# A two-block transformer kernel: merged norms and early context columns, the first expert's products ahead of the gates, squares summed by TensorE, and a store in four parts

## The chip, the core and the metric

The kernel runs on one core of one Trainium2 chip. PE is TensorE (matrix products into PSUM banks), ACT is ScalarE, DVE is VectorE, POOL is GpSimd and SP is SyncE; the last two mostly issue DMAs. The metric is the device time of one execution in microseconds, lower is better. The time before is 1702.18 us, the median of three runs (1700.3 to 1703.35).

## What is computed

A first block over 256 tokens of width 1024, then a second block over these tokens and 256 context tokens. Cut to what matters here:

```python
def rmsnorm(x, g):                       # EPS = 1e-6
    return x * rsqrt(mean(x * x) + EPS) * g

# first block
u = rmsnorm(h, norm_mix); proj = u @ w_in
o_a = forgetting_attention(...); o_b = stick_breaking_attention(...)
h = h + concat(rmsnorm(o_a, norm_fox_out), rmsnorm(o_b, norm_sb_out)) @ w_out
h = h + memory_cross_attention(rmsnorm(h, norm_xattn), rmsnorm(mem, norm_mem))   # 4 heads
h = h + moe(rmsnorm(h, norm_ffn))        # 16 experts of hidden 256: 4 groups of 4,
                                         # best group, 2 best experts in it, all computed
x = rmsnorm(h, norm_final)               # "fin1"

# second block, two layers; the last one needs its output on x alone
for l in range(2):
    shift, scale, gate (two of each) = silu(c) @ w_mod[l] + b_mod[l]       # for x
    the same of c_ctx                                                      # for ctx
    h  = modulate(rmsnorm(x,  g_norm1[l]), sh1,  sc1)     # h*(1+scale)+shift
    hc = modulate(rmsnorm(xc, g_norm1[l]), sh1c, sc1c)
    project both with w_in[l]: Fourier mix, mLSTM (q, k, v, o, gates), latent attention
    ...
    x = x + ga1 * (mix @ w_out[l]); x = x + ga2 * mlp(modulate(rmsnorm(x, g_norm2[l]), ...))
out = rmsnorm(x, g_final)                # "fin2"
```

## The kernel before

Activations are kept transposed: partitions hold 128 of the 1024 features, eight tiles of them, and columns are tokens. `LAT` are the 256 columns of the tokens, `CTX` the 256 of memory or context; the residual `res` holds both. Each engine has its own program, written out by hand; the order in each is the order of the code, and semaphores join them.

Weights come from HBM in 350 pieces of 512 KB over SP's queue into a ring of four slots. Each product is made of three: ACT rounds the piece to `wh` (L532), DVE makes the remainder `wl` (L1568, `split`), and the activations have the same two parts `uh` and `ul`. PE (L995, through `prod`) sums uh*wh, ul*wh and uh*wl.

A norm goes so: ACT squares tiles of `res` (L558) into slots of `sq`, the first into slot 3 and the others in turn into slots 0 and 1; DVE adds each to slot 3 (`add_square`, L1586); PE multiplies slot 3 by a matrix of ones (`norm`), which sums over partitions, with f32 operands; ACT makes the reciprocal root `rstd` by Ln and Exp (L568, L570). Then DVE forms the tiles `uv` (L1608), ACT rounds them to `uh` (L578), and DVE makes the rest `ul` (L1597 or L1599). Around some norms PE has filler matmuls on a tile of ones (`turn_over`, L1039); the table `SPIN` holds their counts before and after each norm.

The modulation vectors are products of one column with a weight matrix. DVE makes them in 48 tiles for layer 0 as dots (L1676 and L1681, `mod_tiles`; each tile is one dot for the context and one for the tokens) of a tile that POOL has loaded. Six stand in the stick-breaking attention, four in the output projection (`MOD_OUT`), four in the cross-attention's query (`MOD_XQ`), two in its output (`MOD_XO`), and 32 in the expert loop, one for each of the 32 half-experts (units).

The router: ACT copies the logits (L717), PE transposes them (L1276), DVE works out the weights, PE spreads them over the partitions with 64 matmuls (`gates`) into two banks that ACT empties (L727), and then the first unit begins. In each unit PE makes gate and up (48 matmuls), and the down product of the unit before.

The hand-over: after the last unit DVE adds four banks to the residual (L1914), adds the bias of the modulation (L1920, L1923), scales the residual by fin1 (L1931), and layer 0's first norm `n1_0` follows over tokens and context. Then PE computes three outputs side by side (`together`): the gates of the mLSTM and its first two heads, 24 steps of three matmuls each, 512 columns wide. ACT copies the head (L793).

In each layer the scans of the mLSTM's gates (`gate_rows`) stand in DVE's program at the third and fourth of the projection's tiles. At the end DVE scales eight tiles (L2266) and SP stores them in one DMA:

```python
            sp.wait_ge(S("norm_out"), normed("fin2")[1])
            sp.dma_start(out, res[:, :, LAT]).then_inc(S("stored"), 16)
```

## Time and profile before

| | us |
|---|---|
| median of 3 runs | 1702.18 |
| the profiled execution | 1705.07 |
| its span in the trace | 1703.2 |
| PE busy | 1619.8 |
| DVE busy | 1077.3 |
| ACT busy | 771.8 |
| POOL busy | 96.6 |

The profiled execution is one run of its own: 1703.2 us of span and 1.87 us around it. A timeline lists what one engine did in order: start, length, engine, line, operation, output<-inputs, how many alike, and in brackets the idle time before with the operation that ended it. Matmuls are pipelined, so the length of one is more than its step to the next: the step is read from two starts. PEclk is the granted clock of PE, 1.00 being 2.4 GHz and 0.50 being 1.2 GHz.

### The profile page before, as it was taken

What the parts mean: (1) busy time and instruction counts of PE and PEld (TensorE: products, weight loads), DVE (VectorE), ACT (ScalarE), POOL (GpSimd) and SP (SyncE); (2) the same over time, 40 slices, a digit from 0 to 9 for tenths busy, and PEclk for the clock granted to TensorE, in tenths of its full rate; (3) what the DMA queues carried; (4) which work ended last, traced back from release to release, by engine and by line L of the source; (5) the groups of instructions that cost most, each with busy time, mean ns of one, the idle gap of its engine ahead of it and who ended that gap; (6) DMA issues with size and microseconds to landing.
All of it is one profiled execution on the core that took longest, in us unless ns stands there. A gap on an engine that the chain in (4) does not pass through costs nothing.

```text
span 1703.2 us, 27364 instructions
## 1 busy us (share of the span) xinstructions
PE 1619.8 (95%) x9992; PEld 1396.6 (82%) x9992; DVE 1077.3 (63%) x1800; ACT 771.8 (45%) x1306; POOL 96.6 (6%) x160
## 2 busy tenths in 40 slices
PE   7999988999999999999889999999999898899997
PEld 7988567899999996775668788888887785799997
DVE  5544677658888887932584755555556944765554
ACT  5544444444444445343462642134323354665562
POOL 0000100000000000000020000000000000100000
PEclk9999999999999999999999999999999999999998
DMA  7633435337777770332114355455542351155552
GB/s 286 203 121 106 119 121 197 126 106 245 244 246 246 244 236 25 99 123 63 34 29 136 136 189 177 142 165 189 166 145 91 112 158 30 45 166 186 173 184 86
DMA packets 70841, 250.96 MB, mean 147 GB/s; under 512 B 7760, under 2 KB 10976, under 8 KB 70640
## 3 DMA queue, kind: packets, MB, share of 16 engines
q1 hardware_dynamic: 54000, 189.43, 33.9%
q0 software_dynamic: 16768, 60.54, 12.5%
q8 instruction: 49, 0.80, 0.2%
q14 instruction: 24, 0.20, 0.0%
HBM read 248.84 MB, written 1.09 MB: 147 GB/s over the span
## 4 chain that ended last, share of the span: by engine, by line
PE 81%; DVE 12%; ACT 3%; issue 3%; DMA 1%; DVEq 0%; SPq 0%; ACTq 0%
PE pair L995 79%; DVE uv L1608 1%; DVE sq L2086 1%; DVE wl L1568 1%; ACT wh L532 1%; DVE sq L1586 1%; DVE small L1635 1%; DVE sq L1644 1%; PE pair L1162 1%; PE pair L1039 1%; DVE uh_f L1681 1%; ACT sq L558 0%; ACT sq L600 0%; DVE ul L1597 0%; DVE spent L1676 0%
## 5 line engine op out<-in xcount | busy, mean ns | idle before, releaser
L995 PE MATMUL pair<-uh,wh 128*128 128x256 f32 (+3 forms) x1840 | 579.0, 315 | 13.1 <-DVE ul L1597 4.5
L1568 DVE TENSOR_TENSOR wl<-ring,wh 128x1024 fp32r<-128x1024 f32 x350 | 426.9, 1224 | 245.0 <-ACT wh L532 237.9
L995 PE MATMUL pair<-uh,wl 128*128 128x256 f32 (+3 forms) x1840 | 574.3, 312 | 0.0
L995 PE MATMUL pair<-ul,wh 128*128 128x256 f32 (+3 forms) x1840 | 572.7, 311 | 0.0
L532 ACT ACTIVATE wh<-ring 128x1024 fp32r<-128x1024 f32 x350 | 367.5, 1052 | 267.9 <-PE pair L995 262.3
L995 PEld LDWEIGHTS pair<-uh,wh 128*128 128x128 f32 (+1 forms) x1840 | 343.5, 187 | 42.6 <-issue 13.8
L995 PEld LDWEIGHTS pair<-uh,wl 128*128 128x128 f32 (+1 forms) x1840 | 343.6, 187 | 25.6
L995 PEld LDWEIGHTS pair<-ul,wh 128*128 128x128 f32 (+1 forms) x1840 | 343.3, 187 | 24.9
L995 PE MATMUL pair<-hh,wh 128*128 128x512 f32 (+1 forms) x512 | 172.7, 337 | 0.8
L995 PE MATMUL pair<-hh,wl 128*128 128x512 f32 (+1 forms) x512 | 172.0, 336 | 0.0
L995 PE MATMUL pair<-hl,wh 128*128 128x512 f32 (+1 forms) x512 | 172.0, 336 | 0.0
L995 PEld LDWEIGHTS pair<-hh,wh 128*128 128x128 f32 x512 | 97.1, 190 | 12.0 <-issue 2.0
L995 PEld LDWEIGHTS pair<-hl,wh 128*128 128x128 f32 x512 | 97.2, 190 | 10.0
L995 PEld LDWEIGHTS pair<-hh,wl 128*128 128x128 f32 x512 | 97.1, 190 | 10.0
L2207 DVE TENSOR_TENSOR hl<-sq,hh 128x512 f32 (+1 forms) x64 | 35.8, 559 | 95.9 <-ACT hh L954 95.8
L949 ACT ACTIVATE sq<-pair 128x512 f32<-128x512 f32 (+1 forms) x64 | 31.3, 489 | 107.4 <-PE pair L995 107.4
L995 PE MATMUL pair<-hidh,wl 128*128 128x256 f32 x256 | 72.6, 284 | 0.0
L995 PE MATMUL pair<-hidh,wh 128*128 128x256 f32 x256 | 72.5, 283 | 0.0
L995 PE MATMUL pair<-hidl,wh 128*128 128x256 f32 x256 | 72.4, 283 | 0.0
L1039 PE MATMUL pair<-spin 128*128 128x512 f32 x250 | 65.9, 414 | 0.0
L995 PE MATMUL pair<-wh,uh 128*128 128x256 f32 (+1 forms) x192 | 57.2, 298 | 3.0 <-ACT qkp L793 3.0
L471 POOL DMA_DIRECT2D uh_f<-in_mods x48 | 36.0, 751 | 418.1 <-DVE macc L1681 267.4
(259 smaller groups left out, 2080.7 us busy)
## 6 DMA issues: line engine op xcount, KB each, us to landing
ring<-in_w_stream SPq DMA_DIRECT2D x350, 512.0 KB, 3.9
uh_f<-in_mods POOLq DMA_DIRECT2D x48, 512.0 KB, 6.1
mod_w<-in_mods POOLq DMA_DIRECT2D x48, 512.0 KB, 3.8
ml<-ml_dram POOLq DMA_DIRECT2D x4, 512.0 KB, 8.1
table<-in_table SPq DMA_DIRECT2D x1, 1849.5 KB, 12.0
res<-in_x SPq DMA_DIRECT2D x4, 256.0 KB, 3.9
res<-in_mem SPq DMA_DIRECT2D x1, 1024.0 KB, 14.3
res<-in_ctx POOLq DMA_DIRECT2D x1, 1024.0 KB, 6.1
```

Of the source, the lines that this page charges most:

```text
L471: pool.dma_start(mod_w[l][g % 2], src).then_inc(S(f"mod_in{g % 2}"), 16)
L532: act.activation(wh[:, s, :], ring[:, s, :], ACT.Copy).then_inc(S("w_hi"), 1)
L949: act.activation(r, bank[(b0 + j) % 4][:, 0:n], ACT.Relu).then_inc(S("job_emptied_act"), 1)
L995: ins = pe.matmul(*operands, **flags)
L1039: pe.matmul(bank[b], spin[:, 0:P], spin[:, :], start=True, stop=True)
L1162: last = pe.transpose(bank[6][:, to * P:(to + 1) * P], prob[i % 2][:, j * P:(j + 1) * P], ident)
L1568: tt(wl[:, s, :], ring[:, s, :], wh[:, s, :].bitcast(F32), ALU.subtract).then_inc(S("w_lo"), 1)
L1586: tt(sq[0:p, 3, 0:n], sq[0:p, 3, 0:n], sq[0:p, t % 2, 0:n], ALU.add).then_inc(S("norm_add"), 1)
L1608: last = stt(o, src, g, r, ALU.mult, ALU.mult)
L1635: dve.tensor_reduce(smv(i, 0, 0, g), b, AX_X, ALU.max, negate=True).then_inc(S("sm_max"), 1)
L1644: last = ts(p, p, smv(i, 1, k), None, ALU.mult)
L2207: tt(hl[:, d, 0:n].rearrange("p a b -> p (a b)"), sq[:, 2 + j % 2, 0:n], hh[:, d, 0:n].rearrange("p a b -> p (a b)").bitcast(F32), ALU.sub ...
```

## The change

1. fin1 and n1_0 are merged. ACT squares the unscaled residual with weights `gsum` = sqrt(g_fin1^2 + eps), and the root takes eps^2 for eps; the tokens' tiles of layer 0 are made of the unscaled residual with `gcomb`, the product of both gains. The true scaling by fin1 (squares, norm on PE, eight scalings on DVE) stands within layer 0's projections. The context's norm `ctx` is made in the router, its tiles `c1_0` at the end of the expert loop, and PE multiplies the context columns while the token norm is formed, then the token columns. The 75 fillers of the hand-over and the 20 of the router go; four are new.
2. The first unit's gate and up products come right behind the router's products, and the transposes behind the twelfth of them. ACT and DVE split the pieces up to the fourth of the experts before the gates are copied.
3. In each norm but the looped ones (`n1_1`, `fin2`) and those of one step, the last square is not added by DVE: PE sums slot 3 and the slot of the last square.
4. Modulation tiles: the last one of the output projection and the last of the cross-attention's output go behind the split that follows the adds; the latter is one more (`MOD_XO` 3), one is new in the cross-attention (`MOD_XAT`), and the expert loop has 30.
5. `gate_rows` stands at the twelfth and fourteenth tile, in both layers.
6. The store is four DMAs of 256 KB, each behind two scalings.

```diff
-SPIN = {"mix": (0, 19, 6), "sb": (5, 5, 6), "xattn": (6, 8, 6), "ffn": (6, 8, 6), "fin1": (24, 0, 4),
-        "n1_0": (34, 17, 5), "n2_0": (7, 17, 5), "n1_1": (18, 17, 6), "n2_1": (5, 8, 5)}
+SPIN = {"mix": (0, 19, 6), "sb": (5, 5, 6), "xattn": (6, 8, 6), "ffn": (6, 8, 6),
+        "n2_0": (7, 17, 5), "n1_1": (18, 17, 6), "n2_1": (5, 8, 5)}
-MOD_OUT, MOD_XQ, MOD_XO = 4, 4, 2
+MOD_OUT, MOD_XQ, MOD_XAT, MOD_XO = 4, 4, 1, 3
...
-            sp.wait_ge(S("norm_out"), normed("fin2")[1])
-            sp.dma_start(out, res[:, :, LAT]).then_inc(S("stored"), 16)
+            for t in range(4):
+                sp.wait_ge(S("fin2_tile"), 2 * t + 2)
+                sp.dma_start(out[:, 2 * t:2 * t + 2, :], res[:, 2 * t:2 * t + 2, LAT]).then_inc(S("stored"), 16)
...
@@ ACT, router @@
+            act.wait_ge(S("ctx_in"), 16)
+            for t in range(4):
+                square("ctx", t, res[:, 2 * t:2 * t + 2, CTX], P, 512)
             act.wait_ge(S("rt_logits"), 1)
...
+            ch.link(act.activation(gsum, tab("g_fin1"), ACT.Square))
+            ch.link(act.activation(gsum, gsum, ACT.Ln, bias=tab("eps")))
+            ch.link(act.activation(gsum, gsum, ACT.Exp, scale=0.5))
+            root("ctx", P, T, D, rstd[:, T:2 * T])
+            split(S_MOE + 4)
             for e in range(NE // 2):
...
-            split(S_MOE + 2)
...
@@ PE, a norm @@
-                for j in range(HALVES[name]):
-                    last = mm(norm_bank(name)[0:p, 0:n], ones[0:p, 0:p], sq[0:p, 3, j * n:(j + 1) * n],
-                              start=(j == 0), stop=(j == HALVES[name] - 1))
+                slots = [3] if name in LOOPED or steps == 1 else [3, (steps - 1) % 2]
+                for slot in slots:
+                    if slot != 3:
+
+                        pe.wait_ge(S("norm_sq"), SQ_AT[name] + steps)
+                    for j in range(HALVES[name]):
+                        last = mm(norm_bank(name)[0:p, 0:n], ones[0:p, 0:p], sq[0:p, slot, j * n:(j + 1) * n],
+                                  start=(slot == 3 and j == 0), stop=(slot == slots[-1] and j == HALVES[name] - 1))
...
@@ PE, router @@
-            turn_over(20, 5)
+            gate_up(0, 0, S_MOE, first=True)
+            norm("ctx", P, T)
+            turn_over(4, 5)
             pe.wait_ge(S("rt_gate"), 1)
...
             pe.wait_ge(S("moe_lo"), 1)
+            pe.wait_ge(S("gate_in"), NE // 2)
...
@@ PE, hand-over @@
+                    for j in range(3):
+                        outs[j] = (outs[j][0](),) + outs[j][1:]
+                        for k in range(3):
+                            half("c1_0", CTX, j, k)
+                    for k in range(3, KT):
+                        if k == 5:
+                            norm("n1_0", P, T)
+                        for j in range(3):
+                            half("c1_0", CTX, j, k)
+                    for k in range(KT):
+                        for j in range(3):
...
+                            last = half("n1_0", LAT, j, k)
...
                 for j in range(2, 8):
 
+                    if l == 0 and j == 4:
+                        norm("fin1", P, T)
...
@@ DVE, the adds to the residual (out1, xo) @@
-                    if s < mods:
+                    if s < mods - 1:
                         mod_tiles(1, spent[:, :, :])
                     if s >= 2:
                         add_square(name, s - 1, P, 512)
                 add_square(name, 3, P, 512)
                 split(first + 7 + AHEAD)
+                mod_tiles(1, spent[:, :, :])
...
@@ DVE, cross-attention @@
+                if i == 1:
+                    mod_tiles(MOD_XAT, spent[:, :, :])
...
@@ DVE, hand-over @@
-            for j in range(KT):
-                stt(res[:, j, LAT], res[:, j, LAT], g[:, j:j + 1], rstd[:, 0:T], ALU.mult,
-                    ALU.mult).then_inc(S("fin1_tile"), 1)
-                if j >= 3:
-                    add_square("n1_0", j - 2, P, 512)
...
@@ DVE, the tiles of a layer @@
                 for j in range(16):
                     split(p0 + j + AHEAD)
-                    if j in (2, 3):
-                        gate_rows(j - 2)
+                    if j < 2:
+                        gate_bias(j)
                     if 2 <= j < 10:
                         conv(j - 2)
+                    if j in (11, 13):
+                        gate_rows((j - 11) // 2)
+                    if l == 0 and j == 1:
+                        add_squares("fin1", 512)
+                    if l == 0 and j == 10:
+                        mod_bias(0)
+                        dve.wait_ge(S("norm_rstd"), NORM["fin1"] + 1)
+                    if l == 0 and 10 <= j < 14:
+                        for k in (2 * j - 20, 2 * j - 19):
+                            stt(res[:, k, LAT], res[:, k, LAT], tab("g_fin1")[:, k:k + 1], sq[:, 2, 0:T], ALU.mult,
+                                ALU.mult).then_inc(S("fin1_tile"), 1)
```

The order on DVE at the hand-over, behind the last dots of the expert loop. Before (`pair` are the PSUM banks, `table` the constants):

```order
L1893 COPY modv<-macc 128x8 [waits mod_used]
L1914 TENSOR_TENSOR res<-pair,res 128x2x256 [waits moe_down,macc_out]
L1914 TENSOR_TENSOR res<-pair,res 128x2x256 [waits moe_down] x2
L1586 TENSOR_TENSOR sq<-sq 128x512 [waits norm_sq]
L1914 TENSOR_TENSOR res<-pair,res 128x2x256 [waits moe_down]
L1586 TENSOR_TENSOR sq<-sq 128x512 [waits norm_add,norm_sq] x2
L1920 TENSOR_TENSOR modv<-modv,table 128x96
L1923 SCALAR_TENSOR_TENSOR gmod<-modv,table 128x16 [waits dve_step] x2
L1931 SCALAR_TENSOR_TENSOR res<-res,table,rstd 128x256 [waits norm_rstd,dve_step]
L1931 SCALAR_TENSOR_TENSOR res<-res,table,rstd 128x256 x3
L1586 TENSOR_TENSOR sq<-sq 128x512 [waits norm_sq]
L1931 SCALAR_TENSOR_TENSOR res<-res,table,rstd 128x256
```

After; L2020 makes a context tile, L1692 a rest, L2039 adds to the residual, L1679 adds squares, L1701 makes a token tile:

```order
L2020 SCALAR_TENSOR_TENSOR uv<-res,gmod,rstd 128x256 [waits norm_rstd,macc_out]
L2020 SCALAR_TENSOR_TENSOR uv<-res,gmod,rstd 128x256
L1692 SCALAR_TENSOR_TENSOR ul<-uv,modv,uh 128x256 [waits u_h]
L2020 SCALAR_TENSOR_TENSOR uv<-res,gmod,rstd 128x256
L1692 SCALAR_TENSOR_TENSOR ul<-uv,modv,uh 128x256 [waits u_h] x2
L2039 TENSOR_TENSOR res<-pair,res 128x2x256 [waits moe_down] x4
L2020 SCALAR_TENSOR_TENSOR uv<-res,gmod,rstd 128x256 x2
L1692 SCALAR_TENSOR_TENSOR ul<-uv,modv,uh 128x256 [waits u_h] x2
L1679 TENSOR_TENSOR sq<-sq 128x512 [waits norm_sq]
L1679 TENSOR_TENSOR sq<-sq 128x512 [waits norm_add,norm_sq]
L2020 SCALAR_TENSOR_TENSOR uv<-res,gmod,rstd 128x256 x2
L1692 SCALAR_TENSOR_TENSOR ul<-uv,modv,uh 128x256 [waits u_h]
```

The dots, the scalings and most square adds are gone from here; context tiles and rests stand on both sides of the residual adds.

PE in the router, from the last product for the logits. Before:

```order
L995 MATMUL pair<-uh,wl 128x256
L1276 MATMUL pair<-table,logit_rows 128x20 [waits rt_rows]
L1276 MATMUL pair<-table,logit_rows 128x20
L1039 MATMUL pair<-spin 128x512 x20
L995 MATMUL pair<-table,small 128x128 [waits rt_gate]
L995 MATMUL pair<-table,small 128x128 x7
L995 MATMUL pair<-table,small 128x128 [waits gate_in]
L995 MATMUL pair<-table,small 128x128 x3
```

After, first around the transposes (L1333), then from the first unit's last product to the third of the gates' banks:

```order
L1040 MATMUL pair<-uh,wl 128x256
L1333 MATMUL pair<-table,logit_rows 128x20 [waits rt_rows]
L1333 MATMUL pair<-table,logit_rows 128x20
L1040 MATMUL pair<-uh,wh 128x256
...
L1040 MATMUL pair<-uh,wl 128x256
L1040 MATMUL pair<-sq,table 128x256 [waits norm_add]
L1040 MATMUL pair<-sq,table 128x256
L1040 MATMUL pair<-sq,table 128x256 [waits norm_sq]
L1040 MATMUL pair<-sq,table 128x256
L1084 MATMUL pair<-spin 128x512 x4
L1040 MATMUL pair<-table,small 128x128 [waits rt_gate]
L1040 MATMUL pair<-table,small 128x128 x7
L1040 MATMUL pair<-table,small 128x128 [waits gate_in]
```

The 48 products of the first unit, of which twelve stand before the transposes, and the context norm have taken the fillers' place.

PE at the hand-over, from the last expert product. Before:

```order
L995 MATMUL pair<-hidh,wl 128x256
L1039 MATMUL pair<-spin 128x512 x24
L995 MATMUL pair<-sq,table 128x256 [waits norm_add]
L995 MATMUL pair<-sq,table 128x256
L1039 MATMUL pair<-spin 128x512 x34
L995 MATMUL pair<-sq,table 128x512 [waits norm_add]
L1039 MATMUL pair<-spin 128x512 x17
L995 MATMUL pair<-uh,wh 128x512 [waits w_lo,u_l,job_emptied_dve]
L995 MATMUL pair<-ul,wh 128x512
```

After, first the start of the context columns, then the norm between them and the next context product:

```order
L1040 MATMUL pair<-hidh,wl 128x256
L1040 MATMUL pair<-uh,wh 128x256 [waits u_l,w_lo]
L1040 MATMUL pair<-ul,wh 128x256
L1040 MATMUL pair<-uh,wl 128x256
...
L1040 MATMUL pair<-uh,wl 96x256
L1040 MATMUL pair<-sq,table 128x256 [waits norm_add]
L1040 MATMUL pair<-sq,table 128x256
L1040 MATMUL pair<-sq,table 128x256 [waits norm_sq]
L1040 MATMUL pair<-sq,table 128x256
L1040 MATMUL pair<-uh,wh 128x256 [waits u_l]
L1040 MATMUL pair<-ul,wh 128x256
```

The first products there are 256 columns wide and wait for context tiles alone; the token norm stands behind the 45th of them.

## Rows read from the trace of the kernel before

**Rows 1.** Page: busy time of the engines; shares of the chain that ended last

```profile
PE 1619.8 (95%) x9992; PEld 1396.6 (82%) x9992; DVE 1077.3 (63%) x1800; ACT 771.8 (45%) x1306; POOL 96.6 (6%) x160
...
PE 81%; DVE 12%; ACT 3%; issue 3%; DMA 1%; DVEq 0%; SPq 0%; ACTq 0%
```

**Rows 2.** PE timeline, start: start us, length us, engine, line, operation, tiles, count [idle, releaser]

```profile
8.12 2.05 PE L995 MATMUL pair<-sq,table 128*128 128x256 f32 x4 [8.12 <-DVE sq L1586]
...
21.41 0.41 PE L995 MATMUL pair<-uh,wl 128*128 128x256 f32 x1
21.63 0.41 PE L995 MATMUL pair<-uh,wh 128*128 128x256 f32 x1
...
22.36 0.28 PE L995 MATMUL pair<-uh,wl 128*128 128x256 f32 x1
22.48 0.28 PE L995 MATMUL pair<-uh,wh 128*128 128x256 f32 x1
```

**Rows 3.** PE timeline at the hand-over from the experts to layer 0

```profile
634.34 5.63 PE L1039 MATMUL pair<-spin 128*128 128x512 f32 x24
641.43 1.13 PE L995 MATMUL pair<-sq,table 128*128 128x256 f32 x4 [1.46 <-DVE sq L1586]
...
657.70 0.47 PE L995 MATMUL pair<-uh,wh 128*128 128x512 f32 x1 [0.95 <-DVE ul L1599]
```

**Rows 4.** DVE timeline at the same place

```profile
636.70 1.89 DVE L1914 TENSOR_TENSOR res<-pair,res 128x512 f32<-128x512 f32 x3
...
654.29 2.47 DVE L1608 SCALAR_TENSOR_TENSOR uv<-res,gmod,rstd 128x256 f32<-128x256 f32 x6 [2.61 <-ACT rstd L570]
```

**Rows 5.** ACT timeline: the copy of layer 0's first head

```profile
674.56 0.58 ACT L793 ACTIVATE qkp<-pair 96x512 f32<-96x512 f32 x1
```

**Rows 6.** PE timeline: squares summed by PE in two other norms

```profile
198.91 1.91 PE L995 MATMUL pair<-sq,table 128*128 128x256 f32 x4
...
779.56 1.99 PE L995 MATMUL pair<-sq,table 128*128 128x512 f32 x2
```

**Rows 7.** DVE timeline before the cross-attention norm, and inside the cross-attention

```profile
257.94 1.22 DVE L1676 CUSTOM_DVE_ANT_1 spent<-uh_f,uv 128x1024 f32<-128x1024 f32 x1
...
260.23 1.49 DVE L1586 TENSOR_TENSOR sq<-sq 128x512 f32<-128x512 f32 x2
...
264.84 1.27 DVE L1608 SCALAR_TENSOR_TENSOR uv<-res,table,rstd 128x256 f32<-128x256 f32 x3 [1.99 <-ACT rstd L570]
...
298.93 0.69 DVE L1635 TENSOR_REDUCE small<-pair 128x2 f32<-128x512 f32 x1
```

**Rows 8.** Router: timelines of DVE (first), ACT (second) and PE (the last three)

```profile
338.55 1.28 DVE L1608 SCALAR_TENSOR_TENSOR uv<-res,table,rstd 128x256 f32<-128x256 f32 x3 [0.71 <-ACT rstd L570]
...
346.20 0.47 ACT L717 ACTIVATE logit_rows<-pair,table 20x256 f32<-20x256 f32 x1 [1.32 <-PE pair L995]
...
352.69 7.58 PE L995 MATMUL pair<-table,small 128*128 128x128 f32 x64 [0.91 <-DVE small L1847]
...
361.06 0.29 PE L995 MATMUL pair<-uh,wh 128*128 128x256 f32 x1
```

**Rows 9.** PE timeline in the projections of layer 1

```profile
1324.60 0.45 PE L995 MATMUL pair<-uh,wh 128*96 128x512 f32 x1 [1.53 <-DVE wl L1568]
...
1343.32 0.47 PE L995 MATMUL pair<-uh,wh 128*128 128x512 f32 x1 [1.71 <-DVE wl L1568]
```

**Rows 10.** DVE timeline at the end; DMA issues: tiles, queue, count, KB, us to landing

```profile
1694.79 3.26 DVE L2266 SCALAR_TENSOR_TENSOR res<-res,table,rstd 128x256 f32<-128x256 f32 x8 [1.75 <-ACT rstd L570]
...
uh_f<-in_mods POOLq DMA_DIRECT2D x48, 512.0 KB, 6.1
res<-in_x SPq DMA_DIRECT2D x4, 256.0 KB, 3.9
...
out_dram<-res SPq DMA_DIRECT2D x1, 1024.0 KB, 4.8
```

**Rows 11.** Busy time by stretch: window, length, each engine, PEclk, DMA share, GB/s

```profile
344.00:345.00 1.00, 1.00 (x6) 1.00 (x6) 0.58 (x3) 0.88 (x1) 0.00 (x0) 0.50 0.00 0
```

262 lines of the change are left out of this document (171 added, 91 removed).

## The prediction

> **What bounds the kernel now.** I read the shares of the chain that ended last first: PE holds 81% of it and DVE 12% [rows 1]. PE is busy for 95% of the span [rows 1], so an edit can win in three ways: take work off PE, fill a stretch in which PE only spins or waits, or shorten the way to the end. I then read PE's timeline from norm to norm. In the products PE steps from one 256-column product to the next in 0.118 us; the same products after the first norm step at 0.213 [rows 2], which is the lower clock. Of all stretches the hand-over from the experts to layer 0 is by far the thinnest: PE ends its last expert product and begins filler at 634.34, and the first real product is at 657.70 [rows 3]. In these 23.4 us PE does two small norms and 75 filler matmuls, while DVE adds the expert output, scales it by the first norm, adds eight squares and forms the first tiles of the second norm [rows 4]. The 72 products of 512 columns that follow end with the copy of the first head's result at 674.56 [rows 5].
>
> **The hand-over.** Removed: the scaling between the two norms, the adds of eight squares of 512 columns, and a second wait on a norm, after which the first tile stands at 654.29 [rows 4]. The context tiles no longer hang on the experts at all; their norm is made at the router. By hand, with the durations of before:
> - DVE ends its last weight split at about 634.1. Three context tiles and their rests take 6 x 0.40, with the rounding on ACT between: 636.9. The four residual adds at 0.61 each (three took 1.89, [rows 4]) end at 639.4.
> - Two tiles, two rests (1.7) and the two square adds, each waiting for ACT, put the second add's end at 643.5; PE sums it and the last square in four matmuls of 0.43 (half of a pair that takes 0.85: its 1.13 less the overlap of the ends, [rows 3]) by 645.2; the root on ACT takes 0.9, to 646.2.
> - Two or three latent tiles at 0.40, rounding 0.42, rest 0.40: PE has its first latent operand at 647.85, where before it was 657.6 [rows 3].
> - PE meanwhile has 72 context products of 0.118, 8.5 us, from 635.6 on, in three pieces with the norm between; they end about 648. The latent half is another 8.5 us: 656.65 against 674.5 at the end of the products of before. That is -17.85. A short stretch at the lower clock, as after the first norm [rows 2], costs back 0.8: **-17.0**. Bounds: -14 if DVE's interleaving costs 3 us more than the sum of durations, -18.
> What is late next is the split of the fourth piece on DVE, about 655.5 by the same reckoning, just ahead of PE. So I see no new wait, but the margin is one microsecond.
>
> **The first norm's real scaling** goes into the projections of layer 0. Its eight DVE operations and squares lie beside PE, which has work there. Only its four PE matmuls are on the path: 4 x 0.43 = **+1.7**.
>
> **Last squares by PE.** Each of these norms saves one DVE add (0.69) and gives PE two more f32 matmuls (0.85 at full clock). Where PE waits for DVE the two nearly cancel. At the start the norm takes PE 2.05 [rows 2]; the new one begins 0.84 sooner and is 1.45 longer: +0.6. The memory norm is bound by PE: +0.85. The forgetting attention's norm runs at the lower clock, 1.91 for the pair [rows 6], less one add and some overlap: +0.9 (-0.6 to +1.7). The compressed query in layer 0 gets one more matmul of 512 columns, which took 1.99 there [rows 6] and 0.85 at full clock: +1.3. The second norm of layer 1 lies where DVE is last: -0.3. The others are taken as nought, from -0.2 to +0.85 each. Together **+3.35**.
>
> **Modulation tiles moved.** Before the cross-attention norm two dots of 1.22 stand ahead of the square adds [rows 7]. Behind the split, the adds move from 260.23 to 257.9, and then adds 1.4, split 1.15 and dots 2.3 give 262.9 for the first tile, which stood at 264.84. The gain is 1.9 at most; DVE still holds the dots ahead of the tile, and PE spins at the lower clock: **-1.2** (-2.2 to 0). Before the router a third tile is new, behind the split. There the first norm tile stands at 338.55, released by ACT's root, and DVE had been idle for 0.71, since its split ended at 337.8 [rows 8]; two dots after the split hold it until 340.3: +1.75, counted in the router below. A new pair of dots goes into the cross-attention, between one division and the next maximum at 298.93 [rows 7]. There DVE and ACT take turns, and PE waits for both: 2 x 1.15 = **+2.2** (1.5 to 3; nought only if PE were the late one, against which speaks that DVE's maxima there follow one another directly).
>
> **The router.** Before: logits leave ACT at 346.20 to 346.7, the gates' weights are ready at 352.6, the 64 broadcast matmuls run from 352.69 to 360.3, and the first expert's 48 products from 361.06 to 366.7 [rows 8]. After: the products for the logits end 1.75 later, at 347.7. PE then does the 48 products (5.7), the context norm (1.7) and 4 fillers (0.9): 356, while the gates' weights come at 352.6 + 1.75 + the context square adds on DVE, about 356.5. Broadcast from 357.0. ACT must first make the context root and two splits (2 x 1.04), to 359.4, and only then copies the two banks that PE has filled. From there PE fills one bank in 0.95 (7.58 / 8, [rows 8]) and the last of six more is copied at 366.6; eight products open the y banks, to 367.65. Before, PE stood at the same point at 366.7. So of the 5.7 us of products put into the gap, all is eaten: 1.75 by the dots, the norm's 1.7, the rest by ACT's order. **+0.9** (0 to +3). No end below nought, since that takes the dots being free, and the row on the root's tile excludes it.
>
> **Gate rows of layer 1** are moved from the third and fourth to the twelfth and fourteenth product tile. In layer 1 PE waits 1.53 and 1.71 for a weight split held behind them [rows 9]; both waits go: **-3.2** (-3.2 to -1). In layer 0 the splits had slack. At tiles 11 and 13 DVE has only its split to make, and their result is needed after the values.
>
> **The store.** Eight last scalings run from 1694.79 to 1698.05; one DMA of 1 MB then takes 4.8 to land [rows 10]. In four, the last 256 KB goes out at the same time. The nearest row for a transfer of that size is the load of the input at 3.9 [rows 10]; it shared the queues with other loads, so I take half a step further: 3.0, **-1.8**, from -0.9 to -2.2. As a note beside the sum: the Trainium skill, "DMA: Bandwidth & Descriptors", section "Anatomy of one DMA — SWDGE (gpsimd) path", has a fixed part of some 2 us and a part by bytes; by it the last quarter would land in 2.6, an estimate (the page gives it for GpSimd's queue, the store goes by SP's), and the term would be -2.2. The same page, "Rules for kernel authors", speaks against splitting, since each DMA has its own fixed cost; with the row of 3.9 the split would still win 0.9, because three of the four run beside DVE's scaling.
>
> **Sum.** -17.0 + 1.7 + 3.35 - 1.2 + 2.2 + 0.9 - 3.2 - 1.8 = -15.05. The profiled execution took 1705.07 us, so it would take 1690.0. The median of the runs, 1702.18, lies 2.9 below it; its counterpart is **1687.1**.
>
> **Rivals.**
> - A, the sum as above, terms within their bounds: 1683.5 to 1691. 0.60.
> - B, the lower clock. 75 fillers go at the hand-over and 16 at the router. The clock falls after thin stretches: the granted clock is 0.50 at 344 to 345, when tiles come singly [rows 11], and after the first norm about 15 products ran at 0.213 instead of 0.118, 1.4 us lost [rows 2]. If that comes up at the hand-over's context products, its latent half and the router, it is 3 x 1.5 more than summed: 1691.6. Against it: real products take the fillers' place in both. 
> - C, PE's first half of each norm is hidden. It may sum slot three while DVE would have been adding, at every norm that I priced at nought or more; five such at 0.85 give 1682.8. For it: DVE's adds stand on the chain ahead of the norms. Against it: at the lower clock a pair takes 1.9. 0.12.
> - E, the hand-over gains less. PE has gaps in its context half since DVE puts the tiles between the residual adds, and the first latent operand comes as late as 652, with the next ones singly behind it: some 8 us of the gain go, 1695. For it: every tile passes DVE, ACT, DVE. Against it: DVE had 3 us more work per norm before and stalled 2.6 for the root [rows 4]. 0.08.
> - D, slower than before. The moved modulation tiles are read by the dots in the middle of chains. If their DMAs, on POOL's queue, land late in the cross-attention, before the router and behind the expert loop, DVE stops there with all that is queued behind it. The rule: one landing of such a tile takes 6.1 [rows 10]; three full ones, 18.3, outweigh 15.05 and give 1705.4. It decides from about 5 us late at each of the three. Against it: POOL's loads run ahead and no dot of before waits for one. 0.03.
>
> **Range and chances.** The likeliest case is A: 1687.0. To leave out no more than 2 in 10, the range takes A, most of B and C and part of E: 1682 to 1695. A measurement of this kernel tells 0.2% (3.4 us) from no change. All but D lie further below than that; a mixture of B and E might stay within it: faster 0.95, same 0.02, slower 0.03.
>
> **What would show it.** In the profile after, PE's first latent product should be near 648 and the copy of the first head near 657; PE's fillers there are gone. The wait of 1.53 and 1.71 in layer 1 [rows 9] should be missing, with no new one at the twelfth tile. The first expert product after the y banks open should be at about 367.6 less what the earlier stages gave. Two dots should stand ahead of a maximum near 299, and PE idle behind them. The store should land about 3 us after its last issue. The prediction is wrong if the clock reads 0.50 for more than 3 us in the hand-over, if the first latent product comes after 650, if DVE waits for a modulation tile, or if splits on DVE fall behind PE in layer 0, where it now scales the residual as well.

## The result, and the profile after

Four runs of the changed kernel took 1674.13, 1674.52, 1675.61 and 1683.07 us, median **1675.07**; before, the median of four is 1702.10. The ratio is 0.9861, interval [0.9836, 0.9886]. The forecast was 1687.1 with a range of 1682 to 1695: the sign was right, the size was not, by 12 us. The profiled execution took 1675.61 us, its span 1673.8, where the sum had 1690.0.

The page of after, busy time and chain, to be held against [rows 1]:

```profile
PE 1600.2 (96%) x10021; PEld 1388.5 (83%) x10021; DVE 1069.2 (64%) x1790; ACT 773.0 (46%) x1315; POOL 96.5 (6%) x160
...
PE 83%; DVE 9%; ACT 3%; issue 3%; DMA 1%; DVEq 0%; SPq 0%; ACTq 0%
```

DVE's share of the chain fell from 12% to 9%, PE's busy time by 20 us, mostly fillers. The hand-over, PE first ([rows 3]), then ACT's copy of the first head ([rows 5]):

```profile
629.50 0.35 PE L1040 MATMUL pair<-uh,wh 128*128 128x256 f32 x1 [1.26 <-DVE ul L1692]
...
637.31 1.99 PE L1040 MATMUL pair<-sq,table 128*128 128x256 f32 x8
638.95 0.47 PE L1040 MATMUL pair<-uh,wh 128*128 128x256 f32 x1
...
642.22 0.38 PE L1040 MATMUL pair<-uh,wh 128*128 128x256 f32 x1
```

```profile
651.15 0.58 ACT L838 ACTIVATE qkp<-pair 96x512 f32<-96x512 f32 x1
```

PE ends its last expert product at 628.1 and idles once, for 1.26 us. It has done 45 context products when the norm comes at 637.31, ends the other 27 at 642.2 and begins the tokens' columns there without a wait. From the last expert product to the head's copy it is 23.1 us, before 40.2: a gain of 17.1 where the sum had 17.0. Some 3.4 us of it ran at the lower clock (PEclk in the last column but two):

```profile
632.00:635.00 3.00, 3.00 (x16) 3.00 (x16) 2.47 (x6) 2.52 (x7) 0.00 (x0) 0.54 0.03 5
```

This low stretch cost nothing. In another trace of the changed kernel (e2, below) the clock is 1.00 through the hand-over. PE waits 0.89 us more there for a context tile, and the head's copy comes 23.1 us after the last expert product (634.20) all the same:

```profile
640.84 0.39 PE L1040 MATMUL pair<-uh,wh 128*128 128x256 f32 x1 [0.89 <-DVE ul L1692]
...
643.44 1.99 PE L1040 MATMUL pair<-sq,table 128*128 128x256 f32 x8
...
648.35 0.39 PE L1040 MATMUL pair<-uh,wh 128*128 128x256 f32 x1
```

```profile
657.29 0.58 ACT L838 ACTIVATE qkp<-pair 96x512 f32<-96x512 f32 x1
```

Ten traces with this hand-over have 23.1 us, four with such a stretch and six without. In all ten the norm begins 9.23 or 9.24 us after the last expert product, just behind the end of DVE's two square adds, here in the profiled execution and in e2:

```profile
635.77 1.48 DVE L1679 TENSOR_TENSOR sq<-sq 128x512 f32<-128x512 f32 x2
```

```profile
641.90 1.48 DVE L1679 TENSOR_TENSOR sq<-sq 128x512 f32<-128x512 f32 x2
```

So DVE sets the pace up to the norm, and a slower PE ahead of it is hidden.

The rest of the places that the prediction names. The first norm ([rows 2]), the forgetting attention's norm with the wait ahead of it (the third row is of before, for comparison; [rows 6] has that norm), and layer 1, where nothing stands between a wait of 1.01 and one of 1.49, so both waits of [rows 9] are gone:

```profile
8.22 3.75 PE L1040 MATMUL pair<-sq,table 128*128 128x256 f32 x8 [8.22 <-DMA table<-in_table]
...
192.98 0.67 PE L1040 MATMUL pair<-qk 64*128 64x256 f32 x2 [0.51 <-DVE sbt L1831]
...
195.80 1.89 PE L1040 MATMUL pair<-sq,table 128*128 128x256 f32 x8
```

```profile
194.75 0.67 PE L995 MATMUL pair<-qk 64*128 64x256 f32 x2 [1.92 <-DVE sbt L1738]
```

```profile
1283.45 0.47 PE L1040 MATMUL pair<-uh,wh 128*128 128x512 f32 x1 [1.01 <-DVE ul L1692]
...
1325.10 0.41 PE L1040 MATMUL pair<-wh,uh 128*128 128x384 f32 x1 [1.49 <-ACT qkp L838]
```

The cross-attention ([rows 7]), DVE and then PE:

```profile
284.71 1.23 DVE L1769 CUSTOM_DVE_ANT_1 spent<-uh_f,uv 128x1024 f32<-128x1024 f32 x1 [1.09 <-DMA uh_f<-in_mods]
```

```profile
289.65 0.58 PE L1214 MATMUL pair<-table,sq 128*128 128x128 f32 x3 [3.01 <-DVE sq L1737]
...
300.30 0.66 PE L1214 MATMUL pair<-table,sq 128*128 128x128 f32 x4 [0.52 <-DVE sq L1737]
```

```profile
296.50 0.66 PE L1162 MATMUL pair<-table,sq 128*128 128x128 f32 x4 [1.99 <-DVE sq L1644]
...
305.81 0.66 PE L1162 MATMUL pair<-table,sq 128*128 128x128 f32 x4 [0.52 <-DVE sq L1644]
```

DVE waits 1.09 us for a modulation tile to land, which no dot did in the trace of before, and PE waits 3.01 for the first probabilities instead of 1.99. But a second trace of the kernel before (e1, below) has such a wait at the same dot:

```profile
284.68 1.23 DVE L1676 CUSTOM_DVE_ANT_1 spent<-uh_f,uv 128x1024 f32<-128x1024 f32 x1 [0.81 <-DMA uh_f<-in_mods]
```

Behind it PE's next wait is 0.52 in both kernels, but from the first probabilities to the products of the last output it takes 14.18 us where before it took 12.84; how much of this is the new tile stands with e8 below. The router ([rows 8]) and the end ([rows 10]):

```profile
352.93 5.74 PE L1040 MATMUL pair<-table,small 128*128 128x128 f32 x48 [0.74 <-ACT gates L746]
359.45 1.18 PE L1040 MATMUL pair<-uh,hidl 128*128 128x256 f32 x8 [0.78 <-ACT gates L746]
```

```profile
1667.50 3.25 DVE L2403 SCALAR_TENSOR_TENSOR res<-res,table,rstd 128x256 f32<-128x256 f32 x8 [1.75 <-ACT rstd L581]
```

```profile
out_dram<-res SPq DMA_DIRECT2D x4, 256.0 KB, 2.6
```

### The profile page after: what moved, and what is told of

Read it like the earlier page. It is cut to its first block, busy times and chain, and to the rows that moved or that the text cites. A ratio compares the mean times of both kernels' runs of the same rounds, so it can differ in the third digit from the quotient of the medians.

```text
span 1673.8 us, 27409 instructions
## 1 busy us (share of the span) xinstructions
PE 1600.2 (96%) x10021; PEld 1388.5 (83%) x10021; DVE 1069.2 (64%) x1790; ACT 773.0 (46%) x1315; POOL 96.5 (6%) x160
## 3 DMA queue, kind: packets, MB, share of 16 engines
HBM read 248.84 MB, written 1.09 MB: 149 GB/s over the span
## 4 chain that ended last, share of the span: by engine, by line
PE 83%; DVE 9%; ACT 3%; issue 3%; DMA 1%; DVEq 0%; SPq 0%; ACTq 0%
PE pair L1040 82%; ACT wh L542 1%; DVE uv L1701 1%; DVE sq L2223 1%; DVE small L1728 1%; DVE sq L1737 1%; DVE wl L1660 1%; PE pair L1214 1%; PE pair L1084 1%; DVE ul L1690 0%; DMA uh_f<-in_mods 0%; ACT sq L611 0%; DVE uh_f L1774 0%; DVE spent L1769 0%; ACT rstd L579 0%
## 5 line engine op out<-in xcount | busy, mean ns | idle before, releaser
L1040 PE MATMUL pair<-uh,wh 128*128 128x256 f32 (+3 forms) x1864 | 583.0, 313 | 14.1 <-DVE ul L1690 8.2
L1040 PEld LDWEIGHTS pair<-uh,wh 128*128 128x128 f32 (+1 forms) x1864 | 347.6, 186 | 42.6 <-issue 14.3
L1040 PEld LDWEIGHTS pair<-uh,wl 128*128 128x128 f32 (+1 forms) x1864 | 347.8, 187 | 23.9
L1040 PEld LDWEIGHTS pair<-ul,wh 128*128 128x128 f32 (+1 forms) x1864 | 347.5, 186 | 23.2
L1774 DVE CUSTOM_DVE_ANT_1 uh_f<-uh_f,uv 128x1024 f32<-128x1024 f32 x48 | 58.5, 1219 | 0.0
```

What stands on the lines that cost most here:

```text
L1040: ins = pe.matmul(*operands, **flags)
L1774: return dve.tensor_tensor_reduce(out=mod_w[l][k], in0=mod_w[l][k], in1=mod_c[l][which], scale=1.0, scalar=0.0, op0=ALU.mult, op1=ALU.add, ...
```

## How the runs are compared: the clock

Two executions of the same kernel differ by 5 us or more in four cases of ten. In 92 runs the kernel before took 1691.0 to 1710.9 us with mean granted clocks of 0.990 to 0.977, and the time goes with the clock: 1.5 us for each 0.001 among these runs, 1.2 among 16 of the changed kernel, with 1.5 us of scatter left. So each experiment below has two results: the mean time, and the time brought to one mean clock, 0.985, with 1.3 us for 0.001. The first says what a kernel is worth, the second roughly what its work costs. The errors of both are those of the mean; that of the rate is not in them. The rate is also too simple. The last 3 us of each of the 20 traces read 0.50 with PE idle, and four stores instead of one take away 2.1 us of such time: that alone raises the mean clock by 0.0006 and moves 0.8 us from the second result to the clock. Where a trace has the place itself, its length there is the better measure.

| kernel | runs | mean us | mean clock | us at 0.985 |
|---|---|---|---|---|
| before | 92 | 1701.0 ± 0.4 | 0.9836 ± 0.0003 | 1699.2 ± 0.2 |
| changed | 16 | 1679.2 ± 0.9 | 0.9856 ± 0.0007 | 1680.0 ± 0.4 |
| before + squares on PE (e3) | 12 | 1701.4 ± 1.0 | 0.9857 ± 0.0008 | 1702.2 ± 0.6 |
| before + shift (e4) | 12 | 1703.4 ± 0.9 | 0.9835 ± 0.0006 | 1701.5 ± 0.5 |
| before, few fillers (e7) | 12 | 1704.6 ± 1.3 | 0.9756 ± 0.0006 | not meant |
| changed, squares undone (e5, e14) | 11 | 1677.7 ± 1.3 | 0.9835 ± 0.0008 | 1675.7 ± 0.5 |
| changed, squares in part (e6, e15) | 10 | 1674.1 ± 0.7 | 0.9859 ± 0.0004 | 1675.3 ± 0.2 |
| part, and fillers (e16) | 6 | 1675.3 ± 2.1 | 0.9863 ± 0.0015 | 1677.0 ± 0.5 |
| changed, tile moved (e8) | 6 | 1682.2 ± 0.8 | 0.9843 ± 0.0006 | 1681.3 ± 0.6 |
| part, tile moved in (e12) | 6 | 1679.4 ± 1.4 | 0.9838 ± 0.0010 | 1677.9 ± 0.3 |
| changed, context behind (e9) | 7 | 1688.8 ± 1.8 | 0.9811 ± 0.0012 | 1683.8 ± 0.5 |
| changed, gate rows back (e10) | 6 | 1685.4 ± 1.6 | 0.9842 ± 0.0011 | 1684.3 ± 0.5 |
| changed, one store (e11) | 6 | 1682.4 ± 2.0 | 0.9843 ± 0.0014 | 1681.6 ± 0.5 |
| changed, only fox by PE (e17) | 6 | 1674.5 ± 1.7 | 0.9853 ± 0.0008 | 1675.0 ± 0.9 |
| changed, only fox by DVE (e18) | 6 | 1684.0 ± 1.2 | 0.9825 ± 0.0008 | 1680.8 ± 0.8 |

## The experiments

**Both kernels again (e1, e2, e13), no edit.**

> The kernel before, unchanged, to see how its clock differs from run to run. The trace of before had PE at the lower clock in three stretches of 6.83 us, from 93.65, 196.05 and 219.94, that the trace of after has not; together with shorter ones they are about 10 of the 12 us by which the forecast missed. Theory P (place): these stretches belong to the program, to where its thin places lie; then all runs have a mean clock of 0.980 and 1700 to 1705 us, and the new trace has the same three. Theory C (chance): they differ from run to run; then some runs reach 0.985 or more and are 8 to 10 us faster, near 1692.

> The changed kernel, unchanged. Four runs of it had clocks of 0.987, 0.987, 0.988 and 0.981, the last 8 us longer than the others. Theory C: the spread comes again, one run in four or more at 0.981 and 1683. Theory P: all at 0.987 and 1674 to 1676, and 0.981 is the exception.

> The changed kernel once more, beside the next two on one chip. Ten runs so far have a mean of 1678.1 and a mean clock of 0.9862, against 1701.1 and 0.9835 of 70 runs of before. If the change holds the clock up by itself, it is 0.9855 or more again; if those ten were lucky, 0.984.

Before: 1701.2 median (1695.7 to 1707.7), clocks 0.980 to 0.987. Changed: 1678.7 and 1680.4, ratios 0.9872 [0.9850, 0.9893] and 0.9875 [0.9846, 0.9904]. In the trace of e1 the stretches at the lower clock lie elsewhere than in the one of before (one near 192 instead of 196, one at 93 half as long, none at 220). So much of them is chance of the execution. The first four runs of the changed kernel had a mean of 1676.8 ± 2.1, the twelve later ones 1679.9. Over all runs the change gives 1701.0 - 1679.2 = **21.8 us** (± 1.0), of which 19.2 at one clock and 2.6 by the clock. The rest of the 27 was the draw. The mean of 1679.2 still lies below the range of the forecast.

**Squares on PE alone, in the kernel before (e3), and a mere delay (e4).** The edit of e3 is part 3 of the change; that of e4:

```diff
-SPIN = {"mix": (0, 19, 6), "sb": (5, 5, 6), "xattn": (6, 8, 6), "ffn": (6, 8, 6), "fin1": (24, 0, 4),
+SPIN = {"mix": (0, 35, 6), "sb": (5, 5, 6), "xattn": (6, 8, 6), "ffn": (6, 8, 6), "fin1": (24, 0, 4),
```

> The kernel before with part 3 alone: the last square of each norm summed by PE. By the sum of the prediction it costs 3.35 us (+0.6, +0.85, +0.9, +1.3, -0.3 and a little at the hand-over): 1705. If PE's denser norms and the shift of 2.7 us that they bring are what takes away the lower clock at 94, 196 and 220, it gains instead: 1702 - 3.0 - 3.7 - 2.4 + 1.8 + 0.85, about 1695.

> The kernel before with 35 instead of 19 fillers behind the first norm: nothing but a delay. 16 more at 0.30 are 4.8, of which 2.04 were idle: everything starts about 2.7 us later. Plain sum: 1702 + 2.7 = 1705. Theory P with place in time as the cause: the stretch at 94 is gone (-3.0), perhaps the ones at 196 and 220 too: 1702 or down to 1696. Theory C: 1705 with the spread of before.

e3: ratio 1.0003 [0.9985, 1.0021]. At one clock it costs 3.0 (the sum had 3.35), but its clock is higher by 0.0021 ± 0.0009, which pays it back. e4: 1.0012 [0.9993, 1.0031]; 2.3 at one clock and no change of the clock. So a mere delay does not raise the clock here.

**Part 3 undone in the changed kernel (e5, e14).**

```diff
-    _add += _steps if _name in LOOPED else max(_steps - 2, 0)
+    _add += _steps if _name in LOOPED else _steps - 1
...
-                elif steps > 2:
-                    pe.wait_ge(S("norm_add"), ADD_AT[name] + steps - 2)
+                elif steps > 1:
+                    pe.wait_ge(S("norm_add"), ADD_AT[name] + steps - 1)
...
-                slots = [3] if name in LOOPED or steps == 1 else [3, (steps - 1) % 2]
+                slots = [3]
...
-                if t == STEPS[name] - 1:
-                    return
```

> The changed kernel with part 3 undone: DVE adds the last square of each norm again. In the kernel before, part 3 alone took 2.9 us more at the same mean clock (1702.0 against 1699.1 at 0.985) but its mean clock was 0.9857 instead of 0.9833, so the mean time was the same. Theory S (the squares on PE hold the clock up): the clock falls from 0.986 to 0.984, at the same clock it is 2 to 3 us faster than the changed kernel (1676.5 at 0.985), mean near 1678. Theory T (the clock is held up by the new hand-over): the clock stays at 0.986 and the mean is 1675. The prediction's sum, without a clock: 3.35 less.

> Part 3 undone once more (six runs so far: 0.9830, and 3.3 us less than the changed kernel at the same clock). Theory S: its clock is again lower than that of the changed kernel by 0.002 or more, and the means are equal. If not, the squares do nothing for the clock, and undoing them gains 3 us in the mean.

Ratios 0.9880 [0.9849, 0.9912] and 0.9846 [0.9821, 0.9871]. At one clock 4.3 less than the changed kernel, and the clock is 0.0021 ± 0.0011 lower: 1.5 less in the mean, within the error. This is what Theory S says, but it is not shown by these two alone. In e14 the clock was 0.9840 beside 0.9847 of e13, taken at the same time, and the mean 4.8 us lower, where Theory S had equal means. e17 and e18 decide it better.

**Part 3 in part (e6, e15).** DVE adds again in four norms, the first one, the memory's, fin1 and that of layer 0's compressed query:

```diff
+BY_DVE = ("mix", "mem", "fin1", "cq_0")
...
-                slots = [3] if name in LOOPED or steps == 1 else [3, (steps - 1) % 2]
+                slots = [3] if name in LOOPED or name in BY_DVE or steps == 1 else [3, (steps - 1) % 2]
...
-                if t == STEPS[name] - 1:
+                if t == STEPS[name] - 1 and name not in BY_DVE:
                     return
```

> The changed kernel with DVE adding the last square again in four norms alone: the first, the memory's, fin1 and the compressed query of layer 0, where PE and not DVE was late in the trace (the first norm grew by 1.8, the memory's by 0.8, the query's by about 1.5, fin1's by 0.85). At the same clock 3 to 5 us less than the changed kernel: 1675. If these places also hold the clock up (Theory S), the mean is no lower than 1677.

> Squares in part once more (five runs so far: 1674.9, clock 0.9854). By its costs at the same clock 1675 to 1676; the mean depends on the clock, 1675 at 0.985 and 1677 at 0.984.

Ratios 0.9846 [0.9820, 0.9872] and 0.9833 [0.9807, 0.9858]. The cost of the squares is gone (4.7 less at one clock) and the clock stays: 1674.1 in the mean, **5 us better than the change** (± 1.1) and 27 better than before.

**Which norm holds the clock (e17, e18).** The same edit with other lists ("fox" is the norm of the forgetting attention):

```diff
@@ e17 @@
+BY_DVE = ("mix", "mem", "sb", "xattn", "ffn", "ctx", "n1_0", "fin1", "cq_0", "n2_0", "n2_1")
@@ e18 @@
+BY_DVE = ("fox",)
```

> The changed kernel with DVE adding the last square in all norms but one: in the forgetting attention's norm alone PE sums it. There DVE's add stood ahead of a step of the stick-breaking attention for which PE waited 1.92 us, 0.51 without it; a stretch at the lower clock between 180 and 205 followed in six of six traces with the add on DVE, and in one of twelve without it. Theory F (this one place holds the clock up): mean clock 0.986 as with all squares on PE, and at the same clock no dearer than with none (1675.7): mean 1674 to 1675. If the clock hangs on the other norms: 0.9835 and 1677.

> The complement: the changed kernel with DVE adding the last square in the forgetting attention's norm alone. Theory F: the mean clock falls from 0.9856 to about 0.9835, the stretch between 180 and 205 is there again in the trace, PE waits 1.9 us ahead of it, and the mean is 1681 to 1683, the worst of all. If the clock hangs on the other norms: 0.9855 and 1680.

Ratios 0.9855 [0.9826, 0.9884] and 0.9915 [0.9888, 0.9941], 9.5 us apart in the mean. The two kernels differ in all norms that were changed, so 9.5 is not the price of one. By this norm alone e17 differs from e5 and e14 (3.2 us, 0.0018 of clock) and e18 from the changed kernel (4.9 us, 0.0031): together 4.3 ± 1.2 us and 0.0025 ± 0.0008. PE ahead of that norm and the clock behind it, e17 and then e18:

```profile
190.20 0.67 PE L1041 MATMUL pair<-qk 64*128 64x256 f32 x2 [0.51 <-DVE sbt L1834]
```

```profile
190.00:197.00 7.00, 6.80 (x29) 4.33 (x29) 5.88 (x11) 3.01 (x5) 0.75 (x1) 1.00 0.36 122
```

```profile
195.46 0.70 PE L1041 MATMUL pair<-qk 64*128 64x256 f32 x2 [1.92 <-DVE sbt L1834]
```

```profile
196.00:203.00 7.00, 7.00 (x16) 4.14 (x16) 4.21 (x7) 2.35 (x4) 0.75 (x1) 0.52 0.40 140
```

With DVE's add in the way PE waits 1.92 us for a step of the stick-breaking attention, and 7 us at 0.52 follow; without it 0.51, and the clock stays at 1.00. From the four matmuls ahead of this wait to the first behind the norm it takes 9.68 us in e18 and 6.28 in e17. Of 20 traces, six have the wait of 1.92, all with the add on DVE, and in each of them 3.4 to 6.8 us at the lower clock begin within 2 us after the wait ends. Twelve have the wait of 0.51, all with the add on PE, and none of them has such a stretch there. The last two, one of each kind (e14 and e3), have 6.8 us at the lower clock from 182 and 181 on, ahead of the step, and no wait at it. So this place is not the only one that can start such a stretch. A second one, of 6.8 to 13.7 us near 215, is in four of the 7 and in six of the 13, and no run here says what brings it.

**Fillers (e7, e16).** e7 takes them from the kernel before; e16 puts six ahead of the first context product, in the kernel of e15.

```diff
@@ e7 @@
-SPIN = {"mix": (0, 19, 6), "sb": (5, 5, 6), "xattn": (6, 8, 6), "ffn": (6, 8, 6), "fin1": (24, 0, 4),
-        "n1_0": (34, 17, 5), "n2_0": (7, 17, 5), "n1_1": (18, 17, 6), "n2_1": (5, 8, 5)}
+SPIN = {"mix": (0, 19, 6), "sb": (5, 5, 6), "xattn": (6, 8, 6), "ffn": (6, 8, 6), 
+        "n2_0": (7, 17, 5), "n1_1": (18, 17, 6), "n2_1": (5, 8, 5)}
...
-            turn_over(20, 5)
+            turn_over(4, 5)
@@ e16 @@
+                    turn_over(6, 5)
                     parts(p0 - 1)
```

> The kernel before without the 75 fillers of the hand-over and with 4 instead of 20 at the router, nothing else. Rival B: without fillers the clock is low when the products come back; three places at 1.5 us or more, 1706.5, and the mean clock falls from 0.983 to 0.980 or below. If the fillers do nothing: 1702 and 0.983. What speaks for the first is the stretch of 3.41 us at the lower clock at 631.7 in the trace of after, where PE had been idle for 1.3 us.

> The kernel of the last run with six fillers of PE ahead of its first context product in the hand-over, where it idled for 1.26 us and where most traces of the changed kernel show 3.41 us at the lower clock from 631.7. If this idle time is what lets the clock fall, the stretch goes, 16 products step in 0.118 instead of 0.213, 1.5 us less than without them and the mean clock 0.001 higher. If the clock falls for what comes after (single tiles), no difference, or 0.1 to 0.3 more for fillers that end late.

e7: 1.0021 [1.0002, 1.0040], 3.7 ± 1.3 us more in the mean. Its trace has 43.9 us from the last expert product to the head's copy, 3.7 more than before. Rival B's mechanism is real: without fillers the clock is low for 24 us of the hand-over, but PE hardly works in them (8 of 24 us), and when the products come back it has risen:

```profile
640.00:664.00 24.00, 7.98 (x15) 4.45 (x16) 17.36 (x40) 11.97 (x23) 0.00 (x0) 0.50 0.00 0
664.00:668.00 4.00, 4.00 (x18) 2.91 (x18) 4.00 (x11) 2.63 (x6) 0.00 (x0) 0.99 0.02 4
```

This is also why the rule of 1.3 us does not hold for e7. e16: the low stretch at the start of the hand-over is gone in its trace (1.00 from 627 to 637, against 0.54 in the changed kernel), but so it is in e15 without fillers. The expectation says that most traces have it; four of ten do. The hand-over takes 23.1 us with the fillers and without them, so fillers of 1.4 us for an idle time of 1.26 gain nothing. e16 is 1.7 dearer at one clock.

**The context columns behind the norm (e9).**

```diff
+                    norm("n1_0", P, T)
                     for j in range(3):
...
-                        if k == 5:
-                            norm("n1_0", P, T)
```

> The changed kernel with PE's token norm ahead of all context products of the hand-over instead of behind the 45th of them. DVE and ACT work as before, so the norm cannot start sooner than the last square (about 637 in the trace of after); the 45 products, 5.3 us, then stand behind it. If the gain of the hand-over is context work hidden under the token norm, this costs 45 x 0.118 = 5.3, less the 0.5 or so by which the norm starts sooner, and PE idles for 9 us, so the clock may be low for another 1.5 to 3: 1683 to 1686 at the mean. If the tiles on DVE were what PE waits for in any case, it costs less than 1.

0.9934 [0.9899, 0.9970]. In the mean +9.6 ± 2.0. By the rate this is 3.8 at one clock and 5.8 by the clock, but the clock is low here while PE idles, where the rate does not hold. The trace has 29.9 us from the last expert product to the head's copy instead of 23.1. These 6.8 are the 45 products, which are the hidden part, and the lower clock in the norm behind the idle time (3.75 us instead of 1.99). The other 2.8 are not placed. PE idles 9.16 us, the clock is low for 10.2 of them and of what follows:

```profile
637.88 3.75 PE L1040 MATMUL pair<-sq,table 128*128 128x256 f32 x8 [9.16 <-DVE sq L1678]
```

```profile
632.00:637.00 5.00, 0.00 (x0) 0.00 (x0) 4.05 (x8) 3.34 (x8) 0.00 (x0) 0.50 0.00 0
637.00:642.00 5.00, 4.12 (x13) 3.44 (x14) 3.25 (x7) 2.59 (x6) 0.00 (x0) 0.55 0.01 3
```

**The gate rows of layer 1 back (e10), and one store (e11).**

```diff
@@ e10 @@
-                    if j in (11, 13):
+                    if l == 0 and j in (11, 13):
                         gate_rows((j - 11) // 2)
+                    if l == 1 and j in (2, 3):
+                        gate_rows(j - 2)
@@ e11 @@
-            for t in range(4):
-                sp.wait_ge(S("fin2_tile"), 2 * t + 2)
-                sp.dma_start(out[:, 2 * t:2 * t + 2, :], res[:, 2 * t:2 * t + 2, LAT]).then_inc(S("stored"), 16)
-            sp.wait_ge(S("stored"), 64)
+            sp.wait_ge(S("fin2_tile"), 8)
+            sp.dma_start(out, res[:, :, LAT]).then_inc(S("stored"), 16)
+            sp.wait_ge(S("stored"), 16)
```

> The changed kernel with the gate rows of layer 1 alone back at the third and fourth tile. The prediction: +3.2, the waits of 1.53 and 1.71 come back. 1682.9 at 0.985, mean 1681. Against it: the bias and the logarithms now stand elsewhere, so only one wait may come back (+1.6).

> The changed kernel with one store of 1 MB at the end. The prediction: +1.8 (0.9 to 2.2). The traces say 2.1: from the last scaling to the end 3.05 instead of 5.15. 1681.7 at 0.985, mean 1680.

e10: 0.9902 [0.9868, 0.9936], 4.3 ± 0.7 at one clock. One wait of 3.35 is back in place of the two of 1.53 and 1.71, and 3.4 us at the lower clock begin with it. Neither is in the kernel before: five traces of it and its variants have no lower clock behind their two waits. So e10 prices the waits in another form:

```profile
1327.70 0.76 PE L1040 MATMUL pair<-uh,wh 128*128 128x512 f32 x1 [3.35 <-DVE wl L1660]
```

e11: 0.9890 [0.9855, 0.9926], 1.6 ± 0.7 at one clock. From the last product of the MLP to the end its trace has 12.2 us, the kernel before 12.1 and the changed one 10.0.

**Modulation tiles elsewhere (e8, e12).** e8 takes the tile out of the cross-attention and doubles one in the query's products; e12, on the kernel of e6, moves the query's last tile into the cross-attention instead.

```diff
@@ e8 @@
-MOD_OUT, MOD_XQ, MOD_XAT, MOD_XO = 4, 4, 1, 3
+MOD_OUT, MOD_XQ, MOD_XAT, MOD_XO = 4, 5, 0, 3
-                if s < MOD_XQ:
-                    mod_tiles(1, spent[:, :, :])
+                mod_tiles(2 if s == 1 else 1, spent[:, :, :])
@@ e12 @@
+MOD_OUT, MOD_XQ, MOD_XAT, MOD_XO = 4, 3, 2, 3
-                if i == 1:
-                    mod_tiles(MOD_XAT, spent[:, :, :])
+                if i in (1, 2):
+                    mod_tiles(1, spent[:, :, :])
```

> The changed kernel with the modulation tile of the cross-attention moved into the query's products, where DVE has room. The prediction priced it at 2.2 us (1.5 to 3). The trace shows PE waiting 3.01 instead of 1.99 there, and a stretch of 3.41 us at the lower clock behind it that the kernel before had in one trace and not in another. By the wait alone 1.0 less: 1678.3 at 0.985; by the prediction 2.2 less: 1677; with the clock 2.5 less.

> The kernel of the run on squares in part (DVE adds the last square in the first norm, the memory's, fin1 and the query of layer 0) with one more edit: the fourth modulation tile of the query's products goes into the cross-attention beside the other, behind its second and third divisions. In the trace of after DVE waits 1.09 us for that tile to land and then makes its dots ahead of the first maximum, and PE waits 3.01 for the first probabilities. If PE waits for these dots, the wait falls by 1.1 + 2.3, to nothing much: 3 us less than 1675, near 1672. If the dots in the third place cost what they gain (they follow the alternation of DVE and ACT), 1674 to 1675.

Both expectations fell. e8: 0.9893 [0.9869, 0.9917], 1.3 dearer at one clock, where 1.0 to 2.2 less was expected. In the new place PE waits 1.13 for a split behind the tile; behind its old place the wait is 0.52, as with it:

```profile
282.10 0.39 PE L1040 MATMUL pair<-uh,wh 128*128 128x256 f32 x1 [1.13 <-DVE wl L1660]
...
303.69 0.66 PE L1214 MATMUL pair<-table,sq 128*128 128x128 f32 x4 [0.52 <-DVE sq L1737]
```

That wait does not say that the tile was free, for the clock was low in this stretch of e8. From the first probabilities to the products of the last output it takes 14.2 us without the tile where a low stretch falls near it (e1, e4, e8), and 13.9 to 14.2 with the tile (ten traces). With no low stretch it takes 12.84 without the tile (before, e3, e7) and 13.93 with it (e14, e17, e18). So the tile costs 1.1 us at the full clock and nothing beside a low stretch. Here e7 and then e18:

```profile
295.76 0.66 PE L1162 MATMUL pair<-table,sq 128*128 128x128 f32 x4 [1.83 <-DVE sq L1644]
...
308.60 1.97 PE L995 MATMUL pair<-sq,vx 128*128 128x256 f32 x8 [0.88 <-DVE uv L1654]
```

```profile
292.63 0.66 PE L1217 MATMUL pair<-table,sq 128*128 128x128 f32 x4 [3.04 <-DVE sq L1740]
...
306.56 1.97 PE L1041 MATMUL pair<-sq,vx 128*128 128x256 f32 x8 [0.88 <-DVE uv L1750]
```

e12: 0.9867 [0.9834, 0.9900], 2.6 dearer at one clock than e6 and e15. The first wait did fall, from 3.01 to 0.96, but the third step lost it: DVE copies an output late, and PE waits 2.33 for it.

```profile
289.67 0.66 PE L1217 MATMUL pair<-table,sq 128*128 128x128 f32 x4 [0.96 <-DVE sq L1740]
...
299.95 2.81 PE L1041 MATMUL pair<-sq,vx 128*128 128x256 f32 x8 [2.33 <-DVE uv L1750]
```

## Why the prediction was right or wrong

At one clock the change gives 19.2 us where the sum had 15.05; the clock gives 2.6 (0.8 of it at the end, where PE idles) where the sum had a loss of 0.8 within the hand-over and rival B more; and the draw of the first runs 5.2. The clock and the draw are the larger half of the miss. Two of the signs of being wrong came as well: the clock was low for more than 3 us in the hand-over, which cost nothing, and DVE waited for a modulation tile.

The stages, as means over four traces of the kernel before (one of them with a delay, one without fillers) and seven of the changed one (e2, e13 and e8 to e11 among them), each left out where its edit lies in the stage:

| stage | the sum | the traces |
|---|---|---|
| up to the first product | +0.6 | +1.4 |
| from there to the output projection | +1.75 | **-4.0** |
| from its end to the first product behind the cross-attention norm | -1.2 | -1.3 |
| the query's products | 0 | +1.2 |
| cross-attention | +2.2 | +1.1 |
| its output and the router | +0.9 | +0.6 |
| hand-over, and layer 0 up to its MLP | -14.0 | -14.1 |
| from there to layer 1's last MLP product | -3.5 | -3.9 |
| the end | -1.8 | -2.2 |
| together | -15.05 | -21.1 |

The second row has the miss, and it spreads most: 208.9 to 216.5 us before, 206.9 to 214.1 after. In it lie the memory's norm and that of the forgetting attention. The query's products are longer because a low stretch falls into them in most of these traces (24.1 us with it, 22.6 without).

- **What failed is the term of the forgetting attention's norm, +0.9, which had no clock.** The prediction took the lower clock at that norm as given (1.91 for a pair, [rows 6]) and looked at the norm alone ("less one add"). The add delayed the stick-breaking step ahead of it, and the lower clock began behind that wait (in six traces of six, and in none of the twelve with the short wait). At the full clock the term is -0.5: the norm's matmuls take 0.95 more, but the wait is 1.41 shorter. With the clock it is -4.3 ± 1.2 (e17 and e18, each against the kernels that differ by this norm alone), and the mean clock is 0.0025 ± 0.0008 higher. Rival B had the mechanism with the sign wrong: it named the real products only as what speaks against it, and it looked for low stretches at the hand-over and the router. In the hand-over four of ten traces have one, and it costs nothing.
- **The hand-over, -17.0: right in size, not in its parts.** 17.1 to the head's copy. The sum had 17.85 without its low stretch and took 0.8 off for it; the stretch cost nothing, and the rest was 0.7 less than summed, so two errors cancel. DVE's square adds set the start of the norm; from there the last context product (642.2) and the first token operand (642.17) come together: the first token product came 14.1 us after the last expert product, by the sum 13.5. e9 shows the hidden context columns. The merging of the two norms was not tried alone. The split of the fourth piece made no new wait that can be told in the trace.
- **fin1's scaling, +1.7: right.** The first three outputs of layer 0 end 17.75 us earlier than before, counted from the last expert product, and the products behind that norm 16.2 earlier.
- **Last squares, +3.35: right in the sum** (3.0 in e3, 4.3 in e5 and e14), **wrong in its terms.** The first norm's +0.6 measured +1.8 in this pair of traces (fillers begin at 11.41 instead of 9.61) and 1.2 as a mean over nine traces with the sum on PE and ten with it on DVE: in eight of the nine PE was held by the landing of the table and not by the add, so the norm began 0.5 sooner and not 0.84. Two terms taken as nought were not: at the hand-over the sum on PE gains 0.95 (24.1 us in e5, e14 and e17, 23.1 elsewhere), and in the router the two norms cost about as much (37.4 to 37.6 us there, 38.2 to 38.5 in the changed kernel).
- **Cross-attention tile, +2.2: half of it.** It cost 1.1 at the full clock and nothing beside a low stretch. The dots take 2.3, but DVE had slack behind them: in the trace of before it waits 1.03 us for PE ahead of its fourth maximum. Behind the third division there was less (e12). The wait for the query's last tile is what rival D described. It is in two of five traces with the kernel before's tiles and in eleven of thirteen with the changed kernel's, and the first probabilities come 6.5 us after the first product of the scores instead of 6.0.
- **Before the cross-attention norm, -1.2: right.** The first product behind it stands 2.2 earlier against the one trace of before and 1.0 against the other (e1), as the clock fell; no run was made of it.
- **Router, +0.9:** from the last products of the cross-attention's output to the first product of the second unit the changed kernel takes as long as before by the one trace and 0.8 longer by the mean of three. ACT's copies set the end, as the sum had it.
- **Gate rows, -3.2: right.** Both waits are gone, and the stage is 3.9 shorter, where this term and the -0.3 of the second norm make 3.5. e10 gives 4.3 ± 0.7 with a low stretch that the kernel before did not have.
- **Store, -1.8: right**, 1.6 ± 0.7 by e11 and 2.2 by the traces. The trace has 3.05 us from the end of DVE's scalings to the end of the span instead of 5.15. The four stores of 256 KB land in 2.6 (median), and the row of 3.9 was the worse guide. The Trainium skill, "DMA: Bandwidth & Descriptors", section "Anatomy of one DMA — SWDGE (gpsimd) path", gives 2.6 by its fixed and its variable part, an estimate for a transfer of this size; the trace agrees, on SP's queue too.

**What stays open.** The stages of the traces sum to 21.1 us, within the error of the 21.8 of all runs, but the second row is a mean over few traces that spread by 7 us. The split of 21.8 into 19.2 and 2.6 hangs on the rate of 1.3 us for 0.001, a mean over stretches with busy and idle PE (e7 and e9 break it). The router and the merged norms have no run of their own. Why e16 was dearer than e15 by 1.7 with six runs is not settled; it is not the hand-over.

## What to carry to other kernels

Ask of each wait on TensorE not only how long it is but what the granted clock does behind it: here 1.4 us more of waiting cost 1.4 us as a wait and 2 to 3 us more by the clock. Ask then whether the stretch at the lower clock is on the path: in the hand-over 3.4 us of it cost nothing. Move a helper's step (a square, a sum) onto the busy engine only where that engine was the one waiting; at least four of these norms paid for it, the hand-over's earned 0.95 us and the forgetting attention's the rest. Before a change is timed to within 1%, time the kernel before a dozen times with its mean clock: four runs gave 27 us, sixteen gave 22.

## What the runs showed that was not expected

The time of one kernel on one core spreads over 20 us (1691.0 to 1710.9 in 92 runs), and the mean granted clock explains most of it, 1.5 us for 0.001 with 1.5 us of scatter left. Where the clock is low while TensorE waits anyway it costs little: the hand-over takes 23.1 us with 3.4 us at the lower clock and without them. And e7 has a mean clock of 0.972 in its trace, which is 2 x 0.028 x 1709 = 96 us at the lower level, against 68 and 47 in the two traces of the kernel before (0.980 and 0.986), and took 3.7 us more in the mean.
